# Eight dense steps of a state-space group moved from behind the transposes and key products to around its norm

## What is computed

```python
z, xbc, dt = split(rmsnorm(x) @ w_in)              # dense projections, D_MODEL = 1024
xs, B, C = split(silu(causal_dwconv(xbc) + bias))  # depthwise conv of width 4
for each chunk of 128 tokens:                      # the kernel's chunk; per group of heads
    S_new = S * decay + B^T (xs * dt * decay_out)  # state update   ("su")
    y     = (C B^T * L) (xs * dt) + decay_in * (C S)   # output       ("y")
y = (y + D * xs) * silu(z)
y = rmsnorm over the group's 256 channels          # the group's norm
```

## Time and profile before

| what | value |
|---|---|
| median of the runs | 3643.44 us |
| the profiled execution, its own time | 3639.24 us |
| span of the profiled execution | 3637.5 us |
| PE, PEld, DVE, ACT, POOL busy | 93%, 89%, 47%, 28%, 27% |
| granted TensorE clock, mean | 0.949 |
| chain that ended last | PE 73%, DVE 14%, issue 4%, ACT 3%, DMA 2%, POOL 2% |
| SSM stage, first to last group start | 1359.0 to 2092.3 us |

### The profile page before, as it was taken

The page is one execution under the profiler, slowest core; times in us unless marked ns, Lnnn a source line. Parts: engine busy times, 40 slices in busy tenths (PEclk is TensorE's granted clock), DMA queues, the critical chain, the costliest instruction groups (busy, mean ns, idle before and its releaser), DMA issues.

```text
span 3637.5 us, 54758 instructions
## 1 busy us (share of the span) xinstructions
PE 3389.9 (93%) x21375; PEld 3234.7 (89%) x21375; DVE 1694.2 (47%) x2656; ACT 1025.1 (28%) x2238; POOL 980.7 (27%) x440
## 2 busy tenths in 40 slices
PE   6899999999789989999999978999989999999998
PEld 4889988898689989999989966999867999999998
DVE  4755565555410048777887843223143341314143
ACT  4332333332321123444444333022231110101010
POOL 3212222212112222111121110223333444444442
PEclk7999999999899999999999989999978999999999
DMA  3110111110032222332232255222221111111111
GB/s 117 55 42 22 43 41 45 43 40 21 22 123 76 75 70 66 90 86 77 83 88 75 67 163 199 76 99 64 87 93 59 47 47 46 47 46 46 47 46 64
DMA packets 339221, 249.59 MB, mean 69 GB/s; under 512 B 13652, under 2 KB 320413, under 8 KB 339029
## 3 DMA queue, kind: packets, MB, share of 16 engines
q1 hardware_dynamic: 323310, 228.32, 21.0%
q10 hardware_dynamic: 15792, 19.60, 1.5%
HBM read 201.57 MB, written 46.78 MB: 68 GB/s over the span
## 4 chain that ended last, share of the span: by engine, by line
PE 73%; DVE 14%; issue 4%; ACT 3%; DMA 2%; POOL 2%; SPq 1%; ACTq 0%; DVEq 0%; PEld 0%; PEldq 0%; POOLq 0%
PE psum L1463 8%; PE psum L1465 8%; PE psum L1464 8%; PE psum L1027 8%; PE psum L1029 8%; PE psum L1028 8%; PE psum L1153 4%; PE psum L1319 2%; PE psum L1321 2%; PE psum L1320 2%; DVE arena L2189 2%; PE psum L1279 1%; PE psum L1144 1%; DMA slab<-in_w_in_dram 1%; PE psum L1525 1%
## 5 line engine op out<-in xcount | busy, mean ns | idle before, releaser
L1027 PE MATMUL psum<-xh,whe 128*128 128x344 f32 x2304 | 786.6, 341 | 27.0 <-POOL wle L2992 23.5
L1028 PE MATMUL psum<-xl,whe 128*128 128x344 f32 x2304 | 754.6, 328 | 0.0
L1029 PE MATMUL psum<-xh,wle 128*128 128x344 f32 x2304 | 753.6, 327 | 0.0
L2992 POOL TENSOR_TENSOR wle<-slab,whe 128x1024 fp32r<-128x1024 f32 x104 | 265.1, 2549 | 1509.7 <-ACT whe L1614 1489.3
L1027 PEld LDWEIGHTS psum<-xh,whe 128*128 128x128 f32 x2304 | 450.3, 195 | 32.3 <-issue 15.9
L1028 PEld LDWEIGHTS psum<-xl,whe 128*128 128x128 f32 x2304 | 450.7, 196 | 0.5
L1029 PEld LDWEIGHTS psum<-xh,wle 128*128 128x128 f32 x2304 | 448.4, 195 | 0.0
L3086 POOL TENSOR_SCALAR wparts<-slab 128x1024 fp32r<-128x1024 f32 x80 | 221.7, 2771 | 501.0 <-POOLq L68 501.0
L1463 PE MATMUL psum<-at,wparts 128*128 128x344 f32 x960 | 308.4, 321 | 5.2 <-DVE r L2901 5.2
L1465 PE MATMUL psum<-at,wparts 128*128 128x344 f32 x960 | 307.1, 320 | 0.0
L1464 PE MATMUL psum<-xlow,wparts 128*128 128x344 f32 x960 | 306.6, 319 | 0.0
(11 more groups left out here) (420 smaller groups left out, 6625.3 us busy)
## 6 DMA issues: line engine op xcount, KB each, us to landing
slab<-in_w_in_dram SPq DMA_DIRECT2D x96, 512.0 KB, 4.0
arena<-d_rows SPq DMA_DIRECT2D x40, 512.0 KB, 5.6
slab<-in_w_ff_up_dram SPq DMA_DIRECT2D x32, 512.0 KB, 4.0
slab<-in_w_ff_down_dram SPq DMA_DIRECT2D x32, 512.0 KB, 3.7
out_dram<-arena SPq DMA_DIRECT2D x24, 512.0 KB, 4.5
arena<-in_state_ssm_dram SPq DMA_DIRECT2D x16, 512.0 KB, 6.4
d_yb<-arena SPq DMA_DIRECT2D x16, 512.0 KB, 4.5
slab<-in_w_ssm_up_dram SPq DMA_DIRECT2D x16, 512.0 KB, 3.7
```

The lines of the kernel that those rows point to most:

```text
L1027: pe.matmul(out, w_hi, a_hi, start=(k == 0), stop=False)
L1028: pe.matmul(out, w_hi, a_lo, start=False, stop=False)
L1029: mm = pe.matmul(out, w_lo, a_hi, start=False, stop=(k == KT - 1))
L2992: pool.tensor_tensor(rounded(wle[slot]), slab[slot][:, :], whe[slot], ALU.subtract).then_inc(wlo_ready, 1)
```

## The change

Of the 144 dense steps of a group, four behind "tx" and four behind "cb" are taken away, and eight come at the group's end: four more in the "norm" fill, and four in a new step "last" between n8 and the first "to" transposes. ACT evacuates by the same table; its calls stay where they are, with a new `evac("last")` behind `evac("norm")`. The sum is 144 again. In the last group (`more` false) nothing changes.

```diff
-        SFILL = {"rw": 8, "tb": 8, "tx": 16, "cb": 24, "scan": 8, "fs": 8, "decode": 0, "norm": 16}
-        SSTEPS = ["rw", "tb", "tx", "cb"] + [f"scan{c}" for c in range(NC)] + ["fs", "decode", "norm"]
+        SFILL = {"rw": 8, "tb": 8, "tx": 12, "cb": 20, "scan": 8, "fs": 8, "decode": 0, "norm": 20, "last": 4}
+        SSTEPS = ["rw", "tb", "tx", "cb"] + [f"scan{c}" for c in range(NC)] + ["fs", "decode", "norm", "last"]
@@ PE, body @@
                 hand(G, "n8", g, lambda bk: (
                     pe.matmul(bk[:, 0:NB], ones[:, :], sq8[:, q * NB:(q + 1) * NB], start=(q == 0), stop=(q == 1))
                     for q in range(2)))
+                fill("last")
                 for p in range(4):
@@ ACT, body @@
                 evac("decode")
                 if more:
                     evac("norm")
+                    evac("last")
                     stanh(g + 1, 4)
                     stanh(g + 1, 5)
```

## The result

| | before | after |
|---|---|---|
| median of 4 runs | 3644.52 us | 3664.61 us (3661.62 to 3668.26) |
| ratio, with its 95% interval | | 1.0055 (1.0037 to 1.0072) |
| span of the profiled execution | 3637.5 us | 3659.9 us |
| SSM stage, first to last group start | 733.0 us | 753.8 us |

The change makes the kernel 20 us slower. The forecast was 8.85 us slower, and 3664.61 lies just above the range. Nearly the whole difference of the two spans, 22.4 us, lies in the SSM stage (20.9 us over seven groups). The stage's own length is the better yardstick: its start lies anywhere between 1359.0 and 1368.9 us in the traces of this case, though no kernel changes anything ahead of it.

A forecast was written before the change was run, and what follows sets the result against it. PE, carrying 73% of the chain that ended last, was taken to bound the kernel. Five groups at +1.55 and two at +0.55 us gave +8.85 us, 3652.3 us on the median; range 3630 to 3664.

The forecast's parts named there:

- A: In the scan, ACT's copy of unit 4 waits for its slab and holds the decays, and DVE: plus 1.4 us, not minus 1.9.
- ACT stands for the whole transfer: At scan2, evacuation and slab issue wait for the same matmul; ACT idles some 3.5 us, the transfer taking 3.75.
- y5's gap: In the scan, PE waits at y5 for DVE's late state: idle 3.4 us, then a low clock costing 1.75 us.
- Rival 1: The copy of unit 4 doesn't hold the decays before DVE's weights(3): 3625 us, chance 0.2.
- Rival 2: No clock fall at y5, POOL's unit 5 product costing DVE under 1 us: 3640 to 3648 us, chance 0.2.
- PE now idles 1.9 us before cb0: Behind tx, four steps fewer gain nothing: cb0 needs the bank DVE frees and starts as before.
- nobody waits behind the copies of the other units: ACT's copies of units 2, 5 and the next unit 0 were to cost nothing.
- PE's part in the late n8: At the norm, PE needs 1.88 us more; n8 another 0.45 us late in five groups, not in two.
- so I take no fall: Before cb0, the clock was to stay high through the 1.9 us idle; a fall would cost PE about 1.75 us.
- rival 3: The idle before cb0 lowers the clock under cb and its fill, 1.75 us in seven groups: 3664 us, chance 0.15.
- the gain behind n8: Four dense steps fill PE's 1.23 us gap; full clock for rw and six dense matmuls: minus 1.05 us a group.
- POOL against DVE: In the scan, POOL's two products cost weights(3) and the convolution 0.4 us more than before; DVE is 1.75 us late.

The follow-up runs named there:

- D: POOL's two products of the sample states issued behind unit 2's low part instead of unit 4's; on the kernel before: 3628.56 us, 0.9952.
- A undone: The change, with ACT's copy of unit 4 put behind the decays instead of in front of them: 3647.68 us, 1.0003.

## Why the prediction was wrong

**Right: the mechanism of A, and its size.** "ACT stands for the whole transfer": 3.56 us of idle against "some 3.5", and 3.82 us from issue to copy against 3.75. weights(3) 1.4 us later than before, against su0 1.85 sooner, is a stretch of 25.4 us; it measured 25.25. y5's gap was forecast at 3.4 us and is 2.7 to 3.0. Undoing it gave 17 us back. Rival 1 is out: the copy does hold the decays, in all seven groups. Rival 2 is out: y5's gap was followed by a low clock in all seven, and unit 5's low part cost DVE 1.1 to 2.1 us (1.95 forecast).

The Trainium skill, DMA: Bandwidth & Descriptors, section Anatomy of one DMA, would have had the transfer take 3.2 us, by an estimate from a fit that the page gives for transfers issued by GpSimd. SP issues this one, so it is no test of the page; the slab landed 3.8 us after its issue, and the row of before was the better price.

**Right: "PE now idles 1.9 us before cb0"** (1.97 us, 1.61 in the first group); that nobody waits behind the copies of the other units; and PE's part in the late n8 (+0.4 us a group from fs to n8, forecast 0.45).

**Wrong: "a gap of 2.14 us in an earlier stage left it at 1.00", "so I take no fall".** This is the step that failed. Its price of 1.75 us stood beside it, and as rival 3. The trace has the fall behind cb0 in five groups of seven, at 12.96 - 11.35 = 1.6 us each: 8.1 us. The repeat of the change has it in three, 5 us. With the filler it is in none, and the kernel is 5.9 us faster than that repeat. The interval of the change against before begins at 1.0037, which is above the 1.0024 of the forecast, so the miss is more than noise.

The stage from which the proof was taken has six such gaps, of 1.57 to 2.38 us, and no fall behind any. Another stage of the same trace of before says otherwise. There PE is idle for 1.73 us in five places, and in four of them the clock falls behind it. The windows of two of these, the first with the fall and the second without:

```profile
2662.00:2665.00 3.00, 2.80 (x4) 1.28 (x5) 0.49 (x2) 0.95 (x4) 3.00 (x4) 0.54 0.00 0
2705.00:2708.00 3.00, 2.67 (x7) 1.27 (x8) 0.49 (x2) 1.67 (x5) 2.89 (x4) 1.00 0.00 0
```

Even the earlier trace rows, with 1.39 and 1.23 us of idle and a low clock under them, spoke against it. Rival 3's 3664 us agrees with the 3664.61 measured, but in part by luck: it had the fall in all seven groups, and left out the next item.

**Mis-sized: the gain behind n8.** The forecast was 1.05 us a group, read from the one group end of the earlier trace rows. That end was the dearest of all: rw to cb0 took 19.8 us behind it. Over the six stretches it took 19.5 to 19.8 us in four, where the clock was still low at rw, and 18.6 and 18.9 in two, where it was back. After the change it takes 18.6 in all. So four group ends gained 0.9 to 1.2 us and two 0 to 0.3, and n8 to rw got 0.15 us longer where nothing was forecast. Over the stage this brought 3.3 us in place of 7.35.

The stage became 20.9 us longer and not 8.85. Of these 12 us the clock under cb is 8.1 and the gain behind n8 is 4.0. The other rows are off by less than 2 us each over the seven groups and cancel. A smaller slip: the prediction's "about 106.5 us instead of 105.2" for a group period starts too high; seven periods of before take 733.0 us, 104.7 each, and those after 107.7.

**Overlooked, without effect on this sum: D.** The step "POOL against DVE" priced by how much POOL's blocks on weights(3) and the convolution would change, 0.4 us, and it measured 0.2 (0.7 and 1.64 us, 0.5 and 1.64 before). It did not ask what they cost in the first place, and that they could be moved. At 17 to 20 us no edit of this case gave more.

**What stays open.** Why the clock falls behind one idle of 1.97 us and not behind the next. The same idle was followed by 1.2 GHz in 5 groups of 7 (the change), 3 (its repeat), 3 (A undone), 4 (POOL moved), 1 (without "last") and 0 (steps from tx alone), and six gaps of 1.57 to 2.38 us in an earlier stage of before never were. The length of the gap alone doesn't decide it. That the low clock costs what the filler gives back rests on three pairs, 5.9, 5.9 and 2.5 us, of which the last is within its own noise. What A costs by itself is open too, since the edit that undoes it costs 9 us on the kernel before.

## What to carry to other kernels

A table that says after which step a tile is evacuated also says what ACT stands behind: move a boundary so that an evacuation and the issue of a transfer wait for the same matmul, and the engine stands for the whole transfer, with all that is queued behind. Before work is taken from a place where PE has no wait, look at what the next bank waits for: if it waits for another engine, the move gains nothing ahead of it, and the idle that opens may cost the clock. One gap elsewhere that did not is no proof; look through all gaps of that length in the trace. A fill put behind a wait can run at the low clock and cost more than it covers. And when one engine's moved work stops paying, look for a second engine's long SBUF operations that run beside the first one's critical ones, and move them to where it has time: here that gave more than all moves of matmuls.

## What the runs showed of the hardware

DVE's operations on two SBUF operands don't slow down beside POOL's, they stand until the POOL operation is over: those shown end 0.02 to 1.1 us after it. POOL's low part takes 2.4 us where DVE is out of the way and each of its products 1.9 to 3.0; DVE's 1.23 and 1.28 us become 1.92 and 2.92 beside them, or 3.40, and even an operation on 8 columns takes 1.85 to 2.36 for its usual 0.22. Operations of DVE that read PSUM kept their 0.42 and 0.69 us, beside POOL too, in every group before and after. The price depends on when DVE arrives, not on its size. It can go the other way: in the earlier trace rows unit 5's low part takes 3.40 us, since it meets a convolution of DVE that is under way. And where POOL has one operation right behind another, the two engines take turns, so that the next of DVE's operations stands as well (3.40, then 1.85 us).

The Trainium skill, SBUF — State Buffer, section Who interferes with whom, says that the two share a pair of ports and that only one can hold it, the other standing until it is released. The traces agree: an operation of 1.28 us stood for 2.1 us and took 3.40.

Filler that computes nothing made the kernel faster: behind 14 transposes, 1.69 us of PE, the clock stayed at 1.00 in all seven groups of three kernels, and cb0 to su0 takes 11.35 us where it takes 12.96 behind a fall. And an idle of 1.73 or 1.97 us of PE was followed by 1.2 GHz at some places and not at others of the same kind, in one execution.
